# Sample attention: keys turned in 32x32 blocks by VectorE instead of by matmuls, and products with the queries stationary

## The chip, the core and the metric

The kernel runs on one core of a Trainium2 chip. The metric is the device time of one execution in microseconds. Engine names follow the profile: PE is the matrix engine (PEld its weight loads), DVE is VectorE, ACT is ScalarE, POOL is GpSimd, SP issues DMAs.

## What is computed

The program is one step of a one-layer decoder: modulation and layer norm, one input projection, four groups of mixers, an output projection, and a mixture of 32 experts. 512 prompt tokens and 8 sample tokens (one new token for each of 8 sequences with 2048 past tokens) go through it. The change touches the attention of the 8 sample tokens alone. In the reference, cut to what matters:

```
# NSA, three branches, for q (4 heads, 64 wide), one query a sequence
s_c = q . compressed_keys - slope * distance        # 64 blocks of 32 tokens
p_c = softmax(s_c);  o_c = p_c . compressed_values
imp = p_c.sum(heads), pairs summed                  # 32 past blocks of 64 tokens
sel = top 16 of imp, blocks 0 and the last two forced
o_s = softmax(q . k[sel] - slope * distance) . v[sel]     # selected pages, 2048 + 1 keys
o_w = softmax(q . k_win - slope * distance) . v_win       # window, 512 + 1 keys
nsa = gate0 * o_c + gate1 * o_s + gate2 * o_w
# DSA
score = sum over 4 index heads of w_h * relu(qi_h . ki)   # 2048 + 1 index keys, 32 wide
sel = top 256 of score
dsa = softmax(q . k[sel] - slope * distance) . v[sel]
```

Both kernels score every key of a sequence and mask with a bias of -1e30 what isn't selected, so no key is gathered by rank.

## The kernel before

Everything here stands in one block, `block_sample_attention`, between two barriers of all engines. Two sequences make a pair (`NPAIR` = 4 pairs, index t). A pair's past tokens lie on the 128 partitions: 64 partitions a sequence, and 32 tokens along the free side of each (the index j; with the new token's row and a row of padding `JP` = 34, `JW` = 10 for the window). `cache` holds the pages of one branch as [128, 4 pairs, 34, 64 key + 64 value numbers]: first the pages of `cache_nsa_slc`, and then, in the same place, those of `cache_dsa_kv`, which POOL gathers once the values of the selected branch have been multiplied (`pv_mm` 2).

Scores of a branch are made by `keys(b, turn, product, aside)` on PE. A chunk is four tiles of 128x128. `turn` multiplies slices of the pages by the identity, so that they lie turned in PSUM (for pages two matmuls a tile, one of each 64 columns of PE, L1926 and L1927); ACT copies the 128x512 result to `KTs` (`evacuate`, L2013, released by `k_t`, and it releases by `k_ev`); `product` then loads each turned tile as the stationary operand and streams the 16 (index: 32) query columns through (L1933, L1921). Scores so stand with tokens on partitions. The four branches are index keys (9 chunks), selected pages (17), window (5), DSA pages (17).

The search for the 256th largest index score (`search(k)`, 16 steps of two bits) runs on DVE: a comparison of all scores with three candidates (L2043), a sum (L2045), a signal (`give`), a small matmul by PE that adds over partitions (`count`, L1904), and six short operations on the result (L2049 to L2056, L2042). In PE's queue nine of these counts stand behind chunks of the selected pages, one in two chunks, and seven behind chunks of the DSA pages. `softmax(b, x, J)` takes column maxima on DVE, has PE turn them and spread their result, and subtracts on DVE; ACT takes the exponential; `values(b, src, J)` multiplies by the values, 132 matmuls for a branch of pages (L1950).

Order on DVE: index scores, compressed branch, block selection, searches 0 to 8, softmax of the selected pages, softmax of the window, searches 9 to 15, `choose`, first result, softmax of DSA, second result. The constants (distances times slopes, masks, tables of the search) are made by POOL at the block's start, and a single semaphore (`s_cst`) tells that all are there.

Of the kernel before, what the change touches and what calls it, by code (L numbers as in the profile page):

```python
# [1691 lines left out]
def block_sample_attention(nc, io, G, ctx, sem, sbt):  # L1692
# [5 lines left out]
    KT = sbt(ctx, "KTs", [128, 2, 512])  # L1698
# [12 lines left out]
    S = scratch(0, 128, NPAIR, JP, 8)  # L1711
    X = scratch(0, 128, NPAIR, JP - 1)
    hit = scratch(0, 128, NPAIR, 3, JP - 1)
# [20 lines left out]
    bias = scratch(1, 128, 2, JP, 8)  # L1734
    biasW = scratch(1, 128, JW, 8)
    biasC = scratch(1, 128, 8)
    QB = scratch(1, 128, 2, NPAIR, 16)
    QIB = scratch(1, 128, NPAIR, 32)
    disti = scratch(1, 128, 3, JP)
    dist = scratch(1, 128, 3, JP)  # L1740
    half = scratch(1, 128, 2)
    halfb = scratch(1, 128, 2)
    gw8 = scratch(1, DEC, DEC, 16)
    gw = scratch(1, 128, DEC, 16)
    wm = scratch(1, 128, NPAIR, 8)
    keyscore = scratch(1, 128, NPAIR, JI)
    vc2 = scratch(1, 128, NPAIR, HD + 1)
    small = sbt(ctx, "as_small", [128, 12, 32])
    mxp, mrow, diag, sums = small[:, 0], small[:, 1, 0:1], small[0:32, 2], small[:, 3]
    rinv = small[:, 4:8]  # L1750
    impT, blkm = small[:, 8, 0:NPAIR], small[:, 8, 8:8 + NPAIR]
    Pc = small[:, 9]
    imp = scratch(0, NPAIR, 2, 40)
    imp64 = scratch(0, NPAIR, 128)
    top8 = scratch(0, NPAIR, 8)
    disti = disti.bitcast(I32)
    gate_d = nc.dram_tensor("sample_gates", (DEC, 12), F32, kind="Internal").ap()

    s_new, idx_in, cache_in, win_in = sem("s_new"), G["idx_in"], [G["slc_in"], sem("as_dsa_in")], sem("as_win_in")
    idx_new, cache_new = sem("as_idx_new"), [sem("as_slc_new"), sem("as_dsa_new")]  # L1760
    s_cst, s_zero2, s_q = sem("as_cst"), sem("as_zero2"), sem("as_q")
    k_t, k_ev, k_mm = sem("as_kt"), sem("as_kev"), sem("as_kmm")
    s_read, s_step, p_step, e_in, e_ok, pv_mm = (sem("as_" + n) for n in ("read", "vstep", "pstep", "ein", "eok", "pv"))
    gate_ok, gate_st, gate_in, one_ok = (sem("as_" + n) for n in ("gate_ok", "gate_st", "gate_in", "one_ok"))
    SEARCH = 16
    early, late = 9, SEARCH - 9
    VW = HD + 2

    tiles_of = [NPAIR * JI // 4, NPAIR * JP // 2, NPAIR * JW // 2, NPAIR * JP // 2]
    first_chunk = [0]  # L1770
    for n in tiles_of:
        first_chunk.append(first_chunk[-1] + n // 4)

    with nc.Block() as block:
        @block.sync
        def _(sp):
            for a in range(2):
                sp.dma_start(keyi[64 * a:64 * a + 1, :, PAST // 64, :],
                             io["out16"][0, a::2, 0].unsqueeze(0)).then_inc(idx_new, 16)
                sp.dma_start(cache[64 * a:64 * a + 1, :, JP - 2, :],  # L1780
                             io["out13"][0, a::2, 0].rearrange("s a d -> s (a d)").unsqueeze(0)).then_inc(cache_new[0], 16)
            sp.dma_start(gate_d, gateR[0:DEC, NT]).then_inc(gate_st, 16)
            sp.wait_ge(gate_st, 16)
            sp.wait_ge(gate_ok, 1)
# [18 lines left out]
        def _(pool):  # L1803
            g = nc.gpsimd
            L = lambda i: plink(pool, i)
            def pages(dst, table, n_sem):
                for t in range(NPAIR):
                    g.indirect_dma_start(dst(t), None, table,
                                         bass.IndirectOffsetOnAxis(ap=idx[:, t:t + 1], axis=0)).then_inc(n_sem, 16)

            L(g.iota(disti[:, 0, 0:32], pattern=[[-1, 32]], base=PAST, channel_multiplier=-32))
            L(g.iota(disti[:, 1, 0:8], pattern=[[-1, 8]], base=512, channel_multiplier=-8))
            L(g.iota(disti[:, 2, 0:1], pattern=[[0, 1]], base=PAST - 31, channel_multiplier=-32))
            L(g.memset(dist[:], 0.0))
            L(g.tensor_copy(dist[:, 0, 0:32], disti[:, 0, 0:32]))
            L(g.tensor_copy(dist[:, 1, 0:8], disti[:, 1, 0:8]))
            L(g.tensor_copy(dist[:, 2, 0:1], disti[:, 2, 0:1]))
            L(g.memset(half[:], 1.0))
# [3 lines left out]
            for i, (n, back) in enumerate(((32, 2048.0), (8, 512.0), (1, 2048.0))):  # L1822
                L(g.tensor_scalar(halfb[:, 0:1], half[:, 1:2], back, None, ALU.mult))
                L(g.tensor_scalar(dist[:, i, 0:n], dist[:, i, 0:n], halfb[:, 0:1], None, ALU.add))
            L(g.tensor_scalar(halfb[:], half[:], 1.0, -BIG, ALU.subtract, ALU.mult))
            for h in range(HEADS):
                for a in range(2):
                    c = 4 * a + h
                    hb = halfb[:, a:a + 1]
                    L(g.tensor_scalar(bias[:, 0, :, c], dist[:, 0, :], -SLOPES[2 * h], hb, ALU.mult, ALU.add))  # L1830
                    L(g.tensor_scalar(bias[:, 1, :, c], dist[:, 0, :], -SLOPES[2 * h + 1], hb, ALU.mult, ALU.add))
                    L(g.tensor_scalar(biasW[:, :, c], dist[:, 1, 0:JW], -SLOPES[2 * h], hb, ALU.mult, ALU.add))
                    L(g.tensor_scalar(biasC[:, c:c + 1], dist[:, 2, 0:1], -SLOPES[2 * h], hb, ALU.mult, ALU.add))

            for x, n in ((bias[:, 0], JP), (bias[:, 1], JP), (biasW, JW)):
                y = x[:, n - 2, :].rearrange("p (s h) -> p s h", s=2)
                L(g.affine_select(out=y, in_=y, compare_op=ALU.is_equal, fill=BIG, base=0,
                                  pattern=[[-64, 2], [0, 4]], channel_multiplier=1))
                L(g.memset(x[:, n - 1, :], BIG))
# [7 lines left out]
            L(g.memset(lead, 1.0))  # L1847
            L(g.affine_select(out=lead, in_=lead, compare_op=ALU.is_equal, fill=0.0, base=0,
                              pattern=[[-64, 2]], channel_multiplier=1))
            L(g.tensor_tensor(lead[:, 0:1], lead[:, 0:1], lead[:, 1:2], ALU.add))  # L1850
            L(g.tensor_scalar(no_key, lead[:, 0:1], -1.0, 3e38, ALU.add, ALU.mult))
# [9 lines left out]
            def ones_column(b, src):  # L1861
                pool.wait_ge(k_t, first_chunk[b + 1])
                L(g.memset(src[:, :, :, HD - 1:HD], 1.0))
                pool.sem_inc(one_ok, 1)
            pool.wait_ge(k_mm, first_chunk[1])
            L(g.memset(win[:, :, JW - 2:JW, :], 0.0))
            pool.sem_inc(s_zero2, 1)
            ones_column(1, cache)
            pool.wait_ge(pv_mm, 2)
            pages(lambda t: cache[:, t, 0:32, :].rearrange("p j x -> p (j x)"),  # L1870
                  io["cache_dsa_kv"][0].rearrange("n (s j) a d -> (n s) (j a d)", s=4), cache_in[1])
            ones_column(2, win)
            ones_column(3, cache)

        @block.tensor
        def _(pe):
            step = [0]

            def take(n=1):
                step[0] += n  # L1880
                pe.wait_ge(s_step, step[0])

            def keys(b, turn, product, aside={}):

                n = tiles_of[b] // 4
                for c in range(n + 1):
                    g = first_chunk[b] + c
                    if c < n:
                        if g >= 2:
                            pe.wait_ge(k_ev, g - 1)  # L1890
                        for u in range(4):
                            m = turn(4 * c + u, lambda q: ps[q, 4 + g % 2, u * 128:(u + 1) * 128])
                        m.then_inc(k_t, 1)
                    if c >= 1:
                        pe.wait_ge(k_ev, g)
                        for u in range(4):
                            m = product(4 * (c - 1) + u, KT[:, (g - 1) % 2, u * 128:(u + 1) * 128])
                        m.then_inc(k_mm, 1)
                    if c in aside:
                        aside[c]()  # L1900
# [14 lines left out]
            def turn_index(n, out):  # L1915
                t, j = divmod(n, JI // 4)
                return pe.transpose(out(slice(0, 128)), keyi[:, t, 4 * j:4 * j + 4, :].rearrange("p j x -> p (j x)"), ident[:])

            def product_index(n, k):
                t, j = divmod(n, JI // 4)  # L1920
                return pe.matmul(ps[:, t, j * 32:(j + 1) * 32], k, QIB[:, t], start=True, stop=True)  # L1921

            def turn_pair(src, J):
                def f(n, out):
                    t, j = divmod(n, J // 2)
                    pe.matmul(out(slice(0, 64)), src[:, t, 2 * j, 0:HD], ident[:], start=True, stop=True)  # L1926
                    return pe.matmul(out(slice(64, 128)), src[:, t, 2 * j + 1, 0:HD], ident[:], start=True, stop=True)  # L1927
                return f

            def product_pair(q, J):  # L1930
                def f(n, k):
                    t, j = divmod(n, J // 2)
# [1016 lines left out]
```

## Time and profile before

| what | value |
|---|---|
| median of 3 runs | 2214.84 us (2213.9 to 2225.81) |
| the profiled execution: its time | 2203.56 us |
| the profiled execution: span | 2201.9 us |
| PE busy | 1687.8 us, 77% of the span |
| DVE busy | 913.8 us, 41% |
| ACT busy, POOL busy | 249.7 us, 264.6 us |
| mean granted clock of PE | 0.852 |

The span runs from the first instruction to the last. A granted clock of 1.00 is 2.4 GHz for PE, 0.50 is 1.2 GHz. The shares are means over stages that come one after the other, each between barriers, so a stage is read alone: what ends last in it sets when the next begins. A row of a group of instructions gives engine, line, shapes, count, time busy and mean duration. In PE's rows each float32 matmul of the program shows as two instructions, so that 132 matmuls are 264 in a count.

### The profile page before, as it was taken

What the parts mean: (1) busy time and instruction counts of PE and PEld (TensorE: products, weight loads), DVE (VectorE), ACT (ScalarE), POOL (GpSimd) and SP (SyncE); (2) the same over time, 40 slices, a digit from 0 to 9 for tenths busy, and PEclk for the clock granted to TensorE, in tenths of its full rate; (3) what the DMA queues carried; (4) which work ended last, traced back from release to release, by engine and by line L of the source; (5) the groups of instructions that cost most, each with busy time, mean ns of one, the idle gap of its engine ahead of it and who ended that gap; (6) DMA issues with size and microseconds to landing.
All of it is one profiled execution on the core that took longest, in us unless ns stands there. A gap on an engine that the chain in (4) does not pass through costs nothing. (4 is left out here: it accounts for less than half of the span.)

```text
span 2201.9 us, 52833 instructions
## 1 busy us (share of the span) xinstructions
PE 1687.8 (77%) x21375; PEld 1212.7 (55%) x21376; DVE 913.8 (41%) x2371; ACT 249.7 (11%) x614; POOL 264.6 (12%) x504
## 2 busy tenths in 40 slices
PE   4999528849777759692799768978979988988664
PEld 3878418738446658442566445645646655655321
DVE  3000475554684432377344223423434333433218
ACT  1000201105444111000000000000000000000000
POOL 0000100021213100000111111111111111111121
PEclk9999759968578675795899988989989999999777
DMA  9731100140600140536599999999998489998983
GB/s 305 264 120 42 52 10 1 41 167 9 267 1 1 39 172 21 168 159 262 226 409 411 414 414 406 400 414 412 410 414 327 172 328 406 412 387 346 415 309 152
DMA packets 131845, 533.24 MB, mean 242 GB/s; under 512 B 19403, under 2 KB 35840, under 8 KB 97266
## 3 DMA queue, kind: packets, MB, share of 16 engines
q1 hardware_dynamic: 110218, 474.66, 54.6%
q0 software_dynamic: 19952, 56.76, 6.9%
q8 instruction: 52, 0.85, 0.2%
q10 hardware_dynamic: 1600, 0.79, 0.1%
q14 instruction: 23, 0.19, 0.0%
HBM read 509.20 MB, written 24.95 MB: 243 GB/s over the span
## 5 line engine op out<-in xcount | busy, mean ns | idle before, releaser
L2699 PE MATMUL ps<-wgu,xTm 128*32 128x256 f32 x10112 | 598.7, 394 | 93.9 <-DMA wgu<-in_moe_wgu 81.3
L2699 PEld LDWEIGHTS ps<-wgu,xTm 128*32 128x32 f32 x10112 | 398.9, 114 | 283.1 <-issue 145.8
L2767 DVE STREAM_TRANSPOSE gs<-ps 128x256 f32<-128x256 f32 x158 | 71.1, 450 | 435.6 <-PE ps L2699 435.6
L2712 PE MATMUL ps<-wd,aT 128*32 128x256 f32 x2528 | 164.9, 404 | 83.7 <-issue 44.3
L2712 PEld LDWEIGHTS ps<-wd,aT 128*32 128x32 f32 x2528 | 93.1, 114 | 152.4 <-issue 126.7
L348 PE MATMUL ps<-hT,w_ring 128*128 128x260 f32 (+2 forms) x768 | 172.8, 387 | 2.0 <-DVE hT L390 2.0
L348 PEld LDWEIGHTS ps<-hT,w_ring 128*128 128x128 f32 (+2 forms) x768 | 140.8, 184 | 32.0 <-issue 4.8
L2793 DVE COPY orow<-ps 128x256 f32 x79 | 33.6, 425 | 205.9 <-PE ps L2712 205.9
L2660 POOL COPY gidx<-rowtok 128x1 int32 (+1 forms) x79 | 14.3, 181 | 827.0 <-DVE xTm L2760 827.0
L2744 ACT ACTIVATE ones<-hx 128x128 f32<-128x128 f32 x79 | 24.5, 310 | 753.1 <-DVE hx L2771 753.1
L2656 POOL DMA_INDIRECT xg<-h_dram,gidx x79 | 78.7, 996 | 64.6 <-POOL gidx L2660 64.6
L2712 PE MATMUL ps<-mixT,aT 128*32 128x256 f32 x1312 | 79.3, 379 | 1.3 <-issue 1.3
L2769 DVE TENSOR_TENSOR hx<-gs,biasT 128x256 f32<-128x256 f32 x158 | 67.2, 425 | 22.9
L2712 PE MATMUL ps<-room,aT 128*32 128x256 f32 x1216 | 73.5, 379 | 3.1 <-issue 3.1
L736 PE MATMUL ps<-par_buf 128*128 128x128 f32 (+1 forms) x480 | 59.8, 286 | 7.5 <-DVE par_buf L1010 5.6
L736 PEld LDWEIGHTS ps<-par_buf 128*128 128x128 f32 x480 | 57.5, 200 | 9.5 <-DVE par_buf L1010 6.5
L2667 POOL DMA_DIRECT2D outbuf<-orow x79 | 59.7, 756 | 22.9 <-DVE orow L2793 15.3
L2712 PEld LDWEIGHTS ps<-mixT,aT 128*32 128x32 f32 x1312 | 50.2, 110 | 22.1 <-issue 1.8
L1462 PE MATMUL ps<-dg,Pw 128*128 128x128 f32 x240 | 44.6, 349 | 20.8 <-ACT dg L1520 16.8
L2712 PEld LDWEIGHTS ps<-room,aT 128*32 128x32 f32 x1216 | 46.4, 110 | 22.9 <-issue 4.5
L1462 PEld LDWEIGHTS ps<-dg,Pw 128*128 128x128 f32 x240 | 38.8, 248 | 36.2 <-ACT dg L1520 23.9
L1926 PE MATMUL ps<-ident,cache 128*64 128x128 f32 x272 | 49.3, 342 | 9.6 <-DMA cache<-in_cache_dsa_kv,blk_idx 9.6
(643 smaller groups left out, 2122.1 us busy)
## 6 DMA issues: line engine op xcount, KB each, us to landing
wgu<-in_moe_wgu SPq DMA_DIRECT2D x128, 2048.0 KB, 25.1
wd<-in_moe_wd SPq DMA_DIRECT2D x32, 2048.0 KB, 34.3
room<-in_moe_wd SPq DMA_DIRECT2D x16, 2048.0 KB, 31.7
mixT<-in_moe_wd SPq DMA_DIRECT2D x16, 2048.0 KB, 31.9
ada_ring<-in_w_ada SPq DMA_DIRECT2D x12, 2048.0 KB, 12.0
w_ring<-in_w_in SPq DMA_DIRECT2D x10, 1024.0 KB, 5.3
outbuf<-orow POOLq DMA_DIRECT2D x79, 128.0 KB, 8.5
outbuf<-zD SPq DMA_DIRECT2D x8, 512.0 KB
```

The costliest lines, as they stand in the source:

```text
L348: mm = pe.matmul(ps[0:w, b + a, 0:HALF], w_ring[:, n % RING_IN, k, i * 128:i * 128 + w], hT[:, k, a * HALF:(a + 1) * HALF], start=(k == 0) ...
L736: m = pe.matmul(ps[:, out_bank, h * w:(h + 1) * w], lhs(h), rhs(h), start=True, stop=True)
L1462: m = pe.matmul(ps[:, 4 + r, k * 128:(k + 1) * 128], P[:, n % 3, r, k * 128:(k + 1) * 128], dg[:, n % 2, r, :], start=True, stop=True)
L1926: pe.matmul(out(slice(0, 64)), src[:, t, 2 * j, 0:HD], ident[:], start=True, stop=True)
L2656: nc.gpsimd.indirect_dma_start(xg[:], None, h_rows, bass.IndirectOffsetOnAxis(ap=idx, axis=0))\
L2667: pool.dma_start(rows4(G["outbuf"][ds(c * SLOTS, SLOTS), :]), orow[:, ds((c & 1) * 256, 256)]).then_inc(r_st, 16)
L2699: m = pe.matmul(ps[32 * c:32 * c + 32, p, 0:256].rearrange("r (s j f) -> r s j f", s=2, j=4), xT[:, k, :], blocks[:, :, p, :, c, :], start ...
L2712: m = pe.matmul(ps[32 * c:32 * c + 32, 6, 0:256], aT[:, k, :], wd[b][k // 4][:, k % 4, 256 * c:256 * c + 256], start=(k == 0), stop=(k == ...
L2744: nc.scalar.activation(sg[p], hx[:, p, 0:4, :], ACT.Sigmoid, scale=1.702).then_inc(sg_ok, 1)
L2767: v.transpose(gs[:, p], ps[:, p, 0:256]).then_inc(gu_ev, 1)
L2769: TT(h, gs[:, p].rearrange("p (a n) -> p a n", a=8), b, ALU.add).then_inc(t_rd, 1)
L2793: v.tensor_copy(orow[:, ds((g & 1) * 256, 256)], ps[:, 6, 0:256]).then_inc(r_ev, 1)
```

## The change

Names: `JK` = 33, `JN` = 9, `WK` = 33*32 = 1056, `WN` = 288. DVE now turns the keys with its transpose of 32x32 blocks, straight from the pages into SBUF (`turn_pages`, one instruction of 128x2112 a pair of sequences; the index keys 128x1056; the window 128x576). A block turn leaves each 32 tokens in their own 32 partitions, so a pair's keys come to lie as four quadrants of 32 partitions (kb). PE holds 32 query columns of a quadrant (`QB`, `QIB`, zeros between them so that the four pairs add up in one accumulation) and streams up to 512 columns of keys, four tiles at the positions (0,0), (32,32), (64,64) and (96,96) of the array, all four writing different partitions of one bank. Scores so stand with (pair, sequence, head) on partitions and tokens along the free side; one maximum a row, and the subtraction goes into ACT's bias. What follows (values, search) wants tokens on partitions, so probabilities and index scores are turned back by DVE. The selected branch is finished ahead of the search, so the DSA gather is released before it. The window's keys are turned in search 0, the DSA pages in searches 8 to 11. Constants come in five portions of `s_cst`. In the diff `parts` is ((0, 512), (512, 512), (1024, 32)), `AFTER_WIN` is 5 and `DSA_FROM` is 8.

```diff
+            def index_product(t):
+                pe.wait_ge(k_t, IDX0 + t + 1)
+                for m, (c0, n) in enumerate(parts):
+                    for kb in range(4):
+                        p = slice(32 * kb, 32 * kb + 32)
+                        x = pe.matmul(ps[p, m, 0:n], QIB[p, 32 * t:32 * t + 32], KT[p, t, c0:c0 + n],
+                                      start=(t == 0), stop=(t == NPAIR - 1), tile_position=(32 * kb, 32 * kb))
+                x.then_inc(k_mm, 1)
+            def key_product(unit, kind, bank, keys, J):
+                t = unit % NPAIR
+                pe.wait_ge(k_t, unit + 1)
+                k4 = keys.rearrange("p (j d k) -> p j d k", d=2, k=32)
+                for m, j0 in enumerate(range(0, J, 16)):
+                    n = min(16, J - j0)
+                    for d in range(2):
+                        for kb in range(4):
+                            p = slice(32 * kb, 32 * kb + 32)
+                            q0 = 256 * kind + 64 * t + 32 * d
+                            x = pe.matmul(ps[p, bank + m, 0:32 * n].rearrange("p (j k) -> p j k", k=32),
+                                          QB[p, q0:q0 + 32], k4[p, j0:j0 + n, d, :],
+                                          start=(t == 0 and d == 0), stop=(t == NPAIR - 1 and d == 1),
+                                          tile_position=(32 * kb, 32 * kb))
+                x.then_inc(k_mm, 1)
...
-            keys(1, turn_pair(cache, JP), product_pair(0, JP), {2 * i + 1: count for i in range(early)})
-            softmax_steps()
-            values(1, cache, JP)
...
+            for k in range(SEARCH):
+                count()
+                if k < NPAIR:
+                    window_product(k)
+                if k == AFTER_WIN:
+                    maximum()
+                if k == AFTER_WIN + 1:
+                    values(2, win, JN)
+                if DSA_FROM <= k < DSA_FROM + NPAIR:
+                    page_product(DSA0 + k - DSA_FROM, 1)
...
-            evacuate(0)
-            exp(0, Pc)
-            evacuate(1)
+                nc.scalar.activation(S[:, 0:n], S[:, 0:n], ACT.Exp, bias=mxc[:, 1:2]).then_inc(e_ok, 1)
...
+            def turn_pages(unit, src):
+                t = unit % NPAIR
+                L(v.transpose(KT[:, 2 * (t % 2):2 * (t % 2) + 2].rearrange("p q n -> p (q n)").rearrange("p (j x) -> p j x", x=HD),
+                              src[:, t, 0:JK, 0:HD]))
+                v.sem_inc(k_t, 1)
...
+            def softmax(n):
+                L(v.tensor_reduce(mxc[:, 0:1], S[:, 0:n], AX.X, ALU.max))
+                give()
+                take()
+                L(v.tensor_reduce(mx32, ps[0:1, 6, 0:128].rearrange("p (k c) -> p c k", c=32), AX.X, ALU.max))
+                give()
+                take()
+                L(v.tensor_copy(mxc[:, 1:2], ps[:, 6, 128:129]))
                 v.sem_inc(e_in, 1)
+            def turn_probabilities(b, n):
+                v.wait_ge(e_ok, b + 1)
+                v.wait_ge(pv_mm, b)
+                L(v.transpose(Pt2[:, 0:n], S[:, 0:n]))
+                v.sem_inc(pt_ok, 1)
...
+            v.wait_ge(k_mm, WIN0)
+            L(v.scalar_tensor_tensor(S, dflat, sl_nsa, scores(3, WK), ALU.mult, ALU.add))
+            s32 = S[:, 0:1024].rearrange("p (j k) -> p j k", k=32)
+            L(TT(s32, s32, Mk.unsqueeze(1).broadcast_to((128, 32, 32)), ALU.add))
+            softmax(WK)
+            turn_probabilities(1, WK)
```

On PE, ahead of the softmax of the selected pages, stood 17 chunks of this kind, with nine counts between them (the first rows, before); `cache` are the pages, `KTs` the turned keys, `zD` the queries, and L1904 is a count of the search.

```order
L1926 MATMUL ps<-ident,cache 64x128
L1927 MATMUL ps<-ident,cache 64x128
L1933 MATMUL ps<-zD,KTs 128x16 x4
L1904 MATMUL ps<-zA 128x12
L1926 MATMUL ps<-ident,cache 64x128
```

In their place stand, in the change, four products of 24 matmuls each (`qN` is where the stationary queries lie now), the block mask (L2005), the maximum (L1965, L1968), and the values right behind:

```order
L1937 MATMUL ps<-KTs,qN 32x512 x16
L1937 MATMUL ps<-KTs,qN 32x32 x8
L2005 MATMUL ps<-zA,zD 32x32 x4
L1937 MATMUL ps<-KTs,qN 32x512 x16
L1937 MATMUL ps<-KTs,qN 32x32 x8
L1937 MATMUL ps<-KTs,qN 32x512 x16
L1937 MATMUL ps<-KTs,qN 32x32 x8
L1965 MATMUL ps<-ident,zD 1x128
L1968 MATMUL ps<-as_small 32x1 x4
L1976 MATMUL ps<-cache,zD 8x65 x132
```

So the counts have left this place, and the values of the selected branch come before the first of them. On DVE, from the block selection to the first search, the change has these rows; L2065 turns pages, L2214 turns the index scores back, L2134 the probabilities.

```order
L2065 STREAM_TRANSPOSE KTs<-cache 128x2112 x2
L2214 STREAM_TRANSPOSE zD<-zA 128x1056
L2216 COPY qN<-ps 128x32
L2217 COPY zD<-zD 128x1
L2218 COPY zD<-zD 128x1
L2219 TENSOR_REDUCE zA<-zD 128x33x4
L2221 TENSOR_SCALAR zA<-zA 128x4
L2225 SCALAR_TENSOR_TENSOR zA<-zD,ps 128x1056
L2228 TENSOR_TENSOR zA<-zA,qN 128x1024
L2122 TENSOR_REDUCE zD<-zA 128x1
L2125 TENSOR_REDUCE as_small<-ps 1x32
L2128 COPY zD<-ps 128x1
```

Before, DVE went from the block selection straight to the first search:

```order
L2182 COPY as_small<-ps 128x4
L2043 TENSOR_TENSOR zA<-zA 128x396
L2045 TENSOR_REDUCE zA<-zA 128x12
L2049 TENSOR_SCALAR zA<-ps 128x12
L2053 TENSOR_SCALAR zA<-ps 128x4
```

The turning of two of the four pairs, the bias, the mask and the maximum have so moved ahead of the search, onto DVE.

## Rows read from the trace of the kernel before

**Rows 1.** Timeline of DVE in the stage: start, duration, engine, line, operation, wait ahead.
```profile
699.94 0.24 DVE L2119 TENSOR_TENSOR zD<-gateR,ident 8x96 f32<-8x96 f32 x1 [0.90 <-PEq L136]
...
729.75 1.32 DVE L2146 TENSOR_SCALAR zD<-zD 128x16 f32<-128x16 f32 x2 [25.04 <-POOLq L1859]
...
784.27 2.11 DVE L2189 SCALAR_TENSOR_TENSOR zA<-ps,as_small,zD 128x272 f32<-128x272 f32 x4
...
906.24 0.73 DVE L2087 COPY mixT<-ps 64x8 f32<-64x8 f32 x4 [0.45 <-PE ps L1913]
```

**Rows 2.** Who waited for whom, 740 to 910 us: total, times, longest.
```profile
DVE zA L2049 <- PE ps L1904: 61.3, 16, 15.5
```

**Rows 3.** Groups by form, 740 to 908 us: busy, mean ns.
```profile
L1927 PE MATMUL ps<-ident,cache 128*64 128x128 f32 x272 | 49.3, 343 | 0.0
```

**Rows 4.** Busy time by stretch: length, PE, PEld, DVE, ACT, POOL, clock, DMA, GB/s.
```profile
704.10:727.90 23.80, 23.80 (x115) 23.50 (x115) 0.57 (x2) 5.37 (x9) 16.97 (x90) 0.50 0.00 1
...
749.50:783.40 33.90, 33.90 (x393) 30.88 (x392) 15.95 (x57) 9.16 (x16) 0.34 (x1) 1.00 0.01 2
841.70:873.60 31.90, 31.90 (x209) 28.99 (x206) 8.39 (x32) 4.78 (x8) 0.00 (x0) 0.50 0.00 1
444.20:449.00 4.80, 4.30 (x66) 3.73 (x66) 0.42 (x1) 0.00 (x0) 0.00 (x0) 0.50 1.05 419
449.20:455.80 6.60, 2.08 (x9) 1.50 (x9) 3.96 (x5) 0.00 (x0) 0.00 (x0) 1.00 0.29 99
...
2132.20:2147.80 15.60, 14.15 (x16) 2.35 (x16) 1.27 (x1) 2.52 (x5) 11.21 (x13) 0.50 0.53 171
```

**Rows 5.** Timeline of POOL, SP and PE at the stage's start.
```profile
701.32 0.57 SPq L1778 DMA_DIRECT2D winidx<-out  x1
...
704.10 1.94 PE L1917 MATMUL ps<-ident,winidx 128*128 128x128 f32 x8 [3.10 <-DMA winidx<-out]
...
722.23 6.96 POOL L1856 MEMSET zA<- 128x1 int32 x45
```

**Rows 6.** Groups by form over the whole trace.
```profile
L2699 PE MATMUL ps<-wgu,xTm 128*32 128x256 f32 x10112 | 598.7, 394 | 93.9 <-DMA wgu<-in_moe_wgu 81.3 <-DVE xTm L2760 10.5 <-issue 0.8
...
L2760 DVE STREAM_TRANSPOSE xTm<-xg 128x256 f32<-128x256 f32 x80 | 35.0, 437 | 8.3 <-DMA xg<-h_dram,rowtok 8.3
```

**Rows 7.** Timeline of PE at four places of other stages.
```profile
343.01 3.57 PE L736 MATMUL ps<-par_buf 128*128 128x128 f32 x16 [2.56 <-DVE par_buf L1010]
...
444.23 3.73 PE L830 MATMUL ps<-vec,ST 64*64 64x64 f32 x64 [0.39 <-DVE ST L1045]
...
627.38 2.08 PE L1445 MATMUL ps<-kI,qI 32*128 32x512 f32 x4
...
911.07 7.13 PE L2362 MATMUL ps<-room,mixT 128*128 128x512 f32 x16
```

**Rows 8.** Timeline of DVE: block selection, first and last; a search step with PE free.
```profile
741.59 0.28 DVE L2167 COPY zA<-ps 4x128 f32<-4x128 f32 x1 [0.52 <-PE ps L1974]
...
744.66 0.41 DVE L2179 COPY zA<-zA 4x64 f32<-4x64 f32 x2
...
780.34 0.17 DVE L2049 TENSOR_SCALAR zA<-ps 128x12 f32<-128x12 f32 x1 [2.08 <-PE ps L1904]
...
783.47 0.17 DVE L2049 TENSOR_SCALAR zA<-ps 128x12 f32<-128x12 f32 x1 [0.95 <-PE ps L1904]
```

**Rows 9.** Timeline of ACT, PE and DVE around the last values.
```profile
897.78 1.11 ACT L2006 ACTIVATE zA<-zA 128x1088 f32<-128x1088 f32 x1 [14.19 <-DVEq L2111]
898.94 5.56 PEld L1950 LDWEIGHTS ps<-cache,zA 128*8 128x8 f32 x251 [3.28 <-ACT zA L2006]
...
905.30 0.17 DVE L2220 RECIPROCAL zA<-ps 128x1 f32<-128x1 f32 x1 [7.61 <-PE ps L1950]
```

**Rows 10.** Timeline of POOL and PE: the DSA gather and the first tile of it.
```profile
800.93 1.08 POOL L1808 DMA_INDIRECT cache<-in_cache_dsa_kv,blk_idx  x1 [19.20 <-PE ps L1950]
...
828.24 0.47 PE L1926 MATMUL ps<-ident,cache 128*64 128x128 f32 x1 [9.55 <-DMA cache<-in_cache_dsa_kv,blk_idx]
```

More of the change, by code:

```diff
@@ L1821, in _ @@
             L(g.tensor_scalar(half[:, 0:1], half[:, 1:2], -1.0, 1.0, ALU.mult, ALU.add))
[L1822 to L1825, printed above, removed]
+            L(g.tensor_scalar(halfb[:, 0:1], half[:, 1:2], float(PAST), None, ALU.mult))
@@ L1832, in _ @@
[L1832 to L1839, printed above, removed]
+                    L(g.tensor_scalar(biasC[:, 4 * a + h:4 * a + h + 1], dist0, -SLOPES[2 * h], halfb[:, a:a + 1],
+                                      ALU.mult, ALU.add))
@@ L1877, in _, with take @@
             step = [0]
-            def take(n=1):
-                step[0] += n
+            def take():
+                step[0] += 1
                 pe.wait_ge(s_step, step[0])
[L1883 to L1900, printed above, removed]
+            def index_product(t):
[6 more added lines that the diff above has]
+                x.then_inc(k_mm, 1)
@@ L1939, in softmax_steps @@
                 take()
-                pe.matmul(ps[:, 6, 128:160], ones[0:32, :], diag, start=True, stop=True).then_inc(p_step, 1)
-                if total:
-                    take()
-                    pe.matmul(ps[:, 6, 160:192], ones[:], sums, start=True, stop=True).then_inc(p_step, 1)
+                for kb in range(4):
+                    m = pe.matmul(ps[32 * kb:32 * kb + 32, 6, 128:129], mx32, minus, start=True, stop=True)
+                m.then_inc(p_step, 1)
             def values(b, src, J):
-                pe.wait_ge(e_ok, b + 1)
+                pe.wait_ge(pt_ok, b)
@@ L2191, in _ @@
[L2191 to L2202 removed]
+            v.wait_ge(k_mm, SLC0 + 1)
@@ new lines, in _ @@
+            between = {0: window_turns}
+            for t in range(NPAIR):
+                between[DSA_FROM + t] = lambda t=t: dsa_turn(t)
+            between[AFTER_WIN + 1] = lambda: turn_probabilities(2, WN)
+            for k in range(SEARCH):
+                search(k, between.get(k))
+                if k == AFTER_WIN:
+                    v.wait_ge(k_mm, DSA0)
+                    L(v.scalar_tensor_tensor(S[:, 0:WN], distW.rearrange("p j k -> p (j k)"), sl_nsa, scores(0, WN),
+                                             ALU.mult, ALU.add))
+                    softmax(WN)
@@ L2212, in _ @@
             results(2)
-            v.wait_ge(k_mm, first_chunk[4])
-            v.wait_ge(pv_mm, 3)
-            for t in range(NPAIR):
-                L(TT(S[:, t], ps[:, t, 0:8 * JP].rearrange("p (j c) -> p j c", c=8), bias[:, 1], ALU.add))
-                L(TT(S[:, t], S[:, t], keyscore[:, t, 0:JP].unsqueeze(2).broadcast_to((128, JP, 8)), ALU.add))
-            softmax(3, S, JP)
+            v.wait_ge(k_mm, DSA0 + NPAIR)
+            L(v.scalar_tensor_tensor(S, dflat, sl_dsa, scores(3, WK), ALU.mult, ALU.add))
+            L(TT(S, S, MT, ALU.add))
+            softmax(WK)
+            turn_probabilities(3, WK)
             v.wait_ge(pv_mm, 4)
@@ L2222, in _ @@
             results(4)
+AFTER_WIN = 5
+DSA_FROM = 8
 SLOTS = 32
```

435 lines of the change are left out of this document (230 added, 205 removed).

## The prediction

> **What bounds the kernel now.** I first placed the stage in the span with DVE's timeline: it runs from 699.94 to 906.97 us, 207 us [rows 1], and ends at a barrier, so what it loses or gains moves everything behind it by as much. Then I asked who is waited for. The search's 16 reads of the count (L2049) waited 61.3 us for PE, one of them 15.5 us [rows 2]. A search step whose count meets an idle PE takes 783.47 - 780.34 = 3.13 us, of which DVE waits 0.95 [rows 8]; 16 of them would be 50 us. PE by contrast is busy without a gap in the stretches of page chunks, 33.9 of 33.9 us and 31.9 of 31.9, while DVE works about half and a quarter of them [rows 4]. Turning by the identity alone shows 272 instructions on each of two column halves for 49.3 us [rows 3]. So PE bounds the page stretches, DVE with its exchanges the rest, and in between the stage waits for the DSA gather: PE sat 9.55 us until it landed at 828.24 [rows 10]. At the start DVE stood 25.04 us, for POOL's last constant by name [rows 1], but PE's index chunks filled the same time (23.8 of 23.8 us) [rows 4], so the constants alone cost next to nothing.
>
> The granted clock is part of the price. The same page chunks ran at 1.00 (2.4 GHz) in one stretch and at 0.50 (1.2 GHz) in another, both with PE busy throughout [rows 4].
>
> **Prices.** DVE: a block turn of 128x256 takes 0.437 us [rows 6], an operation of 12 columns 0.17 [rows 8], so (0.437 - 0.17)/244 = 1.09 ns a column. That gives 2.5 us for a turn of 2112, 1.3 for 1056 columns (turn, sum, maximum or bias), 0.8 for 576, 0.5 for 288. No row turns 2112 columns; I find no reason for another slope.
>
> PE: a page product is, in PE's own instructions, 8 passes of 512 columns on each of the four tiles, and 4 of 32. A 512-column pass of the whole array takes 7.13/16 = 0.45 us at full clock; the experts' four column tiles at once take 598.7/10112 x 4 = 0.24 us for 256 columns, 0.47 for 512 [rows 6, 7]; two row tiles at once at half clock take 2.08/2 = 1.0 us [rows 7]. If the four tiles run together, a product costs 8 x 0.45 to 0.47, and some 0.3 for the short ones: 4.0 us at full clock, and about 8 at half. An index product is half of that, a window product (4 passes of 288 columns) 1.1 and 2.3.
>
> Do four tiles in different rows and columns of the array run together when they write one bank? The nearest rows are matmuls of 64x64 tiles at (0,0) and (64,64) into one bank (L830): 64 passes of 64 columns in 3.73 us, 58 ns each. One whole-array pass of 128 columns at the same clock took 3.57/16 = 0.22 us, half of it for 64 columns is 0.11 [rows 7]. So two of them ran at a time. I take the same for four.
>
> The Trainium skill says otherwise: by TensorEngine Tiling (Array Packing), Restrictions and Gotchas, different row tiles cannot access the same PSUM bank simultaneously. The two tiles of L830 speak against it, at other partitions of the bank; no row here shows four. By the rule the products would take turns, which is the third case below.
>
> **The path of the change**, at full clock during products, in trace times of before.
>
> 1. Index keys. SP issues their second row at 701.32 now, and PE starts 2.8 us later [rows 5]. The row moves ahead of a selected one (0.6 us): about 703.5. Four turns of 1.3 us and their links, 708.9. Meanwhile POOL: its short memsets cost 6.96/45 = 0.155 us [rows 5], 32 of them and four long ones make the tables ready near 707, the compressed bias near 712, the distances (two ramps of 256 and 1024, up to 3 us) near 719, everything near 730. DVE is there at 710, 712, 730 and 738, so POOL costs nothing unless it is 8 us late. The compressed softmax passes PE three times behind an index product of 2 (half clock: 4) us: index done at 722.5.
> 2. Selected pages. PE: 723 + two products = 731, the mask, two more, 740.5. DVE beside it: second page turned 725, index scores out 726.5, block selection 3.5 us [rows 8] 730, two turns 735, scores turned back and summed, 738.5. So PE ends last, by 2 us.
> 3. Bias, mask, maximum: three passes over 1056 columns, 4.0; two exchanges with PE 1.7; the exponential 1.11 (1088 columns now [rows 9]) and a hand-over, 1.4; turned back 1.3: 748.9. The 132 matmuls of values stay as they are, 898.94 to 905.30, 6.4 us [rows 9]: 755.3. Before, they ended at 800.5, 0.4 ahead of the gather's issue [rows 10].
> 4. The gather's first tile came 27.7 us after that [rows 10]: now 783.0. DVE gets to search 8 after eight steps of 3.13 us, the window's softmax (3.0) and its turn (0.5): 784.3. The two meet, so the 9.55 us wait is gone, and 1.3 us is all the slack.
> 5. Searches 8 to 11. The next count stands behind a page product, so a step costs product + 0.5 instead of 3.13: first turn 2.5, a first product partly at half clock 6.5, then 4.5 each: 807.3. Four short steps, 817.7.
> 6. `choose` with its exchange 5; mask turned 2.6; first result 2.7; bias, mask, maximum 4.0; exchanges 1.7; exponential 1.4; turn 1.3; values 6.4; last result 906.97 - 905.30 = 1.7 [rows 1, 9]. Sum 26.8: 844.5.
>
> That is 62.5 us ahead of 906.97. The sum leaves out small hand-overs; as an estimate, about 100 of them are new or moved, at 0.03 to 0.05 each like the gaps between DVE's rows, so I take 57. Of it, before and after: to the first result on selected pages (800.5 to 755.3) 45, the rest by the gather's wait and the shorter DSA stretch. Nothing outside the stage changes. 2203.56 - 57 = 2146.6 for a profiled execution; the median of the three runs stands 11.3 above that execution, so 2214.84 - 57 = 2158.
>
> Costed at nothing: ACT's 16 small copies of queries (0.2 each, from 700.6, not wanted before 723); the window's four turns (3.2 us) lie beside the values in search 0; if values came sooner, they would cost that.
>
> **The rivals.** (a) *Full clock in dense products*, as above. After L830, dense for 3.7 us on two diagonal tiles, the clock went from 0.50 to 1.00 [rows 4, 7].
>
> (b) *Half clock throughout.* Four 32x32 tiles are a quarter of the array. A single small tile streamed 14.15 of 15.6 us and stayed at 0.50, and page chunks stayed there for 31.9 us [rows 4]. Then PE is the bound: pages end at 758 instead of 740.5 (+17.5, with the index products), searches 8 to 11 cost 2.5 + 4 x 8.5 = 36.5 instead of 23 (+13.5). Gain 57 - 31 = 26, with the first products perhaps quicker 29: 2186.
>
> (c) *The four tiles take turns* (the other side). A product is then 32 passes of 0.47 and short ones, 15.6 us even at full clock. Index products 30 us, done at 735; pages until 797.5 (+57); window steps +6; searches 8 to 11 67 instead of 23 (+44). 57 - 107 = 50 slower: 2265. This decides as soon as a page product takes over 4 + 57/8 = 11 us, since eight of them lie on the path. The Trainium skill's rule named above asks for this case.
>
> (d) *DVE's turns cost double* for pages read in runs of 64, 5 us each: pages +5 behind PE, searches +8, index +5: gain about 38, inside the span of (a) and (b). With a POOL table late as well it might shrink to nothing.
>
> **Chances.** (a) 0.54, (b) 0.33, (c) 0.05, (d) 0.08. The number is (a)'s: 2158; its own range 2142 to 2174. For 8 in 10 both (a) and (b) must be in: 2138 to 2190. 0.5% is 11 us, about what three runs tell apart here. Faster: all of (a) and (b), most of (d), 0.92; same 0.03; slower 0.05.
>
> **What would show it.** Stage 145 us long instead of 207. Four passes of 512 columns starting within a few hundredths, L1937 busy near 4 us for 24 matmuls; 8 at clock 0.50 is (b), 15 is (c). DVE's L2065 near 2.5 us. POOL's second gather issued near 756, and DVE waiting little or not at all for it at search 8. L2080 waiting 0.95 in searches 1 to 5 and 12 to 15. Wrong I would be above all by the clock, or if the turns or the waits on POOL's five portions put DVE behind PE.

## The result and the profile after

The changed kernel takes 2138.3 us (median of 4 runs, 2135.87 to 2141.68) against 2215.47 for the kernel before on the same chip: ratio 0.963, 95% interval [0.958, 0.968]. That is 77 us less, where 57 were forecast. The time stands at the very bottom of the range (2138); as a ratio, 0.963, it is just below it (2138 / 2214.84 = 0.965). Profiled execution against profiled execution it is 2203.56 to 2135.92, 67.6 us.

All of it comes from the stage. I measure it from DVE's first instruction in the block to its last: 207.0 us before [rows 1], 138.7 after (704.05 to 842.72). What is left of the execution's time, called the rest below, is 1996.5 and 1997.3.

DVE's timeline of the changed kernel at the places that answer to [rows 1, 8, 10] (start, duration, engine, line, operation, wait ahead):

```profile
704.05 0.22 DVE L2137 MEMSET qN<- 128x192 f32 x1 [0.97 <-PEq L136]
...
716.85 0.19 DVE L2165 TENSOR_TENSOR as_small<-ps,zD 128x32 f32<-128x32 f32 x1 [1.64 <-POOLq L1854]
...
722.07 0.19 DVE L2174 TENSOR_TENSOR as_small<-as_small,ps 128x32 f32<-128x32 f32 x1 [3.69 <-PE ps L1990]
...
734.37 4.90 DVE L2065 STREAM_TRANSPOSE KTs<-cache 128x2112 f32<-128x2112 f32 x2 [0.18 <-PE ps L1937]
...
744.33 1.31 DVE L2225 SCALAR_TENSOR_TENSOR zA<-zD,ps 128x1056 f32<-128x1056 f32 x1 [1.41 <-PE ps L1937]
...
785.52 2.38 DVE L2065 STREAM_TRANSPOSE KTs<-cache 128x2112 f32<-128x2112 f32 x1 [1.26 <-DMA cache<-in_cache_dsa_kv,blk_idx]
790.37 2.38 DVE L2065 STREAM_TRANSPOSE KTs<-cache 128x2112 f32<-128x2112 f32 x1
...
807.23 0.17 DVE L2080 TENSOR_SCALAR zA<-ps 128x12 f32<-128x12 f32 x1 [1.91 <-PE ps L1952]
809.96 0.17 DVE L2080 TENSOR_SCALAR zA<-ps 128x12 f32<-128x12 f32 x1 [0.54 <-PE ps L1952]
812.88 0.17 DVE L2080 TENSOR_SCALAR zA<-ps 128x12 f32<-128x12 f32 x1 [0.75 <-PE ps L1952]
...
841.98 0.74 DVE L2118 COPY mixT<-ps 64x8 f32<-64x8 f32 x4 [0.45 <-PE ps L1961]
```

A turn of 128x2112 costs 2.38 us. The long waits for the count (61.3 us, [rows 2]) are gone; 10.6 us are left (total, times, longest, 704 to 843 us):

```profile
DVE zA L2080 <- PE ps L1952: 10.6, 12, 1.9
```

DVE waits 1.26 us for the gather, so the search just meets it. The first two DSA turns start 4.85 us apart (the second and the third 5.40, the last two 4.85), and DVE works through all of it but short waits: it sets the pace there, as e5 shows below.

PE's timeline of the same execution (answers to [rows 7, 9]):

```profile
726.92 7.32 PE L1937 MATMUL ps<-KTs,qN 32*32 32x512 f32 x96
...
752.41 6.15 PE L1976 MATMUL ps<-cache,zD 128*8 128x65 f32 x264 [2.92 <-DVEq L2135]
...
761.73 1.17 PE L1937 MATMUL ps<-kvT,qN 32*32 32x288 f32 x16
...
764.66 2.14 PE L1937 MATMUL ps<-kvT,qN 32*32 32x288 f32 x16
...
788.01 5.08 PE L1937 MATMUL ps<-KTs,qN 32*32 32x512 f32 x48 [3.03 <-DVEq L2067]
...
793.34 3.76 PE L1937 MATMUL ps<-KTs,qN 32*32 32x512 f32 x48
```

Two page products take 7.32 us, 3.7 each. The same window product takes 1.17 or 2.14 us, and the first DSA product 5.08 where the next takes 3.76. Busy time by stretch goes with it (columns as in [rows 4]; the clock stands ahead of the last two). The first row is that of two page products, the second that of searches 0 to 8 with the window's products, the third that of the DSA products behind the first:

```profile
726.90:734.20 7.30, 7.30 (x104) 2.34 (x96) 6.44 (x22) 0.00 (x0) 4.80 (x44) 1.00 0.70 280
...
758.90:784.30 25.40, 13.14 (x159) 7.33 (x159) 17.83 (x62) 0.53 (x1) 4.59 (x5) 0.59 0.94 380
...
790.80:807.20 16.40, 14.79 (x188) 5.47 (x180) 12.62 (x24) 0.00 (x0) 0.33 (x1) 1.00 0.01 2
```

The products of the selected pages, and those of the DSA pages from the second on, ran at 1.00. Between them the mean clock was 0.59: the first two window products ran at 1.00, the last two at 0.50. The first DSA product (788.0 to 793.1) had 0.73.

### The profile page after: what moved, and what is told of

The parts are those of the page before. It is cut to its first block and busy times, and to the rows that moved or that the text cites. A ratio compares the mean times of both kernels' runs of the same rounds, so it can differ in the third digit from the quotient of the medians.

```text
span 2133.6 us, 51812 instructions
## 1 busy us (share of the span) xinstructions
PE 1622.6 (76%) x20898; PEld 1116.4 (52%) x20899; DVE 936.7 (44%) x2347; ACT 224.8 (11%) x582; POOL 266.1 (12%) x515
## 5 line engine op out<-in xcount | busy, mean ns | idle before, releaser
L2757 PE MATMUL ps<-wgu,xTm 128*32 128x256 f32 x10112 | 607.1, 398 | 100.4 <-DMA wgu<-in_moe_wgu 88.0
L2802 ACT ACTIVATE sg<-hx 128x128 f32<-128x128 f32 x79 | 24.4, 309 | 266.2 <-DVE hx L2829 266.2
## 6 DMA issues: line engine op xcount, KB each, us to landing
wd<-in_moe_wd SPq DMA_DIRECT2D x32, 2048.0 KB, 34.4
```

Source lines behind the costliest of these rows:

```text
L2757: m = pe.matmul(ps[32 * c:32 * c + 32, p, 0:256].rearrange("r (s j f) -> r s j f", s=2, j=4), xT[:, k, :], blocks[:, :, p, :, c, :], start ...
L2802: nc.scalar.activation(sg[p], hx[:, p, 0:4, :], ACT.Sigmoid, scale=1.702).then_inc(sg_ok, 1)
```

## The experiments

The stage's length is read as above, each in the profiled execution of its kernel.

| kernel | median us | ratio to before, interval | stage us |
|---|---|---|---|
| changed kernel | 2138.3 | 0.963 [0.958, 0.968] | 138.7 |
| e1 tiles one after the other | 2343.5 | 1.061 [1.055, 1.068] | 344.6 |
| e2 old products, new order | 2216.5 | 1.004 [1.000, 1.008] | 208.2 |
| e3 new products, search first | 2162.3 | 0.980 [0.974, 0.986] | 162.3 |
| e4 second index product earlier | 2138.9 | 0.968 [0.963, 0.974] | 139.2 |
| e5 turns twice | 2158.0 | 0.971 [0.965, 0.978] | 157.0 |
| e6 filler | 2139.3 | 0.963 [0.956, 0.969] | 141.0 |
| e7 four moves of order | 2131.5 | 0.959 [0.954, 0.964] | 134.7 |
| e8 four in a row | 2138.4 | 0.962 [0.956, 0.968] | 139.0 |
| e9, e10 before again | 2207.9, 2211.4 (one run each) | | 207.1, 212.9 |
| e11 e7, DSA turns from search 9 | 2131.5 | 0.961 [0.957, 0.966] | 131.9 |

**e1: do the four tiles run side by side?**

```diff
-                for m, j0 in enumerate(range(0, J, 16)):
-                    n = min(16, J - j0)
-                    for d in range(2):
-                        for kb in range(4):
+                for kb in range(4):
+                    for m, j0 in enumerate(range(0, J, 16)):
+                        n = min(16, J - j0)
+                        for d in range(2):
```

(and `kb` outermost in the index product).

> The changed kernel with the same matmuls in another order: all of tile (0,0), then all of (32,32), and so on, so that neighbours in PE's queue are never on different tiles but at three borders. If four tiles only run together because they alternate in the queue, a page product costs 24 matmuls in turn, about 8 x 4 passes of 0.45 us and 16 short ones, near 15 us at full clock instead of the 3.75 measured: index products +5 each on the path (+20), four page products +47, window +6, searches 8 to 11 about +11 each (+45), so about 115 us more than the changed kernel, near 2250, slower than before. This is also what rival (c) gave for the change itself. If instead the short product of 3.75 us came from cheap small tiles and not from running side by side, or if the queue lets later tiles overtake, the order doesn't matter: within 5 us of the changed kernel's 2138.

It took 205 us more, where 115 were expected. PE's timeline (the first row is an index product, the second two page products less three records, the third a window product, the last a DSA product):

```profile
705.92 8.86 PE L1923 MATMUL ps<-KTs,qN 32*32 32x512 f32 x24
...
743.57 54.92 PE L1937 MATMUL ps<-KTs,qN 32*32 32x512 f32 x93
...
873.81 2.16 PE L1937 MATMUL ps<-kvT,qN 32*32 32x288 f32 x16
...
897.19 27.74 PE L1937 MATMUL ps<-KTs,qN 32*32 32x512 f32 x48 [3.06 <-DVEq L2067]
```

and busy time by stretch:

```profile
897.20:924.80 27.60, 27.60 (x48) 6.10 (x48) 4.35 (x8) 0.00 (x0) 0.00 (x0) 0.50 0.00 1
```

The same 48 instructions take 27.7 us and not 3.7. A factor of four is the turn-taking; the other two is the clock, 0.50 though PE was busy without a gap. The sum had only the first factor. So in the changed kernel the tiles do run together, into one bank. With a single small tile at work the clock stayed at 0.50; the page products with four at work had 1.00.

**e8: how many may stand in a row?** (`kb` and `d` exchanged, so that a tile gets four instructions in a row.)

> The changed kernel with another order of the matmuls of a page product: within a block of 512 columns both halves of the key on one tile, then the next tile. Each tile so gets four instructions in a row, and not two; with all twelve pairs of a tile in a row the product took 27.7 us and not 3.75, but the window's product of four in a row took no longer than before. If the instructions of a tile wait in a queue of its own that holds four, four in a row cost nothing: 3.75 us a product, 2138. If tiles only run together when neighbours in the queue differ, or when the whole queue of about four holds all of them, a product takes 1.5 to 2 times as long at least (6 to 8 us): 4 x 2.5 on the pages and as much in searches 8 to 11, 10 to 30 us slower.

```profile
737.33 7.46 PE L1937 MATMUL ps<-KTs,qN 32*32 32x512 f32 x96 [2.27 <-DVEq L2067]
```

7.46 for 7.32, and 2138.4 for 2138.3 in the median: four in a row cost next to nothing. One rule fits all four shapes: a tile's instructions wait for their tile, up to four of them, and the next tile's begin once no more than four stand ahead. Four in a row: side by side (e8, and e1's window, 2.16 us). Six in a row at half clock: a tile works 3.5 us, the next begins when two of 0.85 are through, 3.5 + 3 x 1.8 = 8.9 (8.86 measured). Twelve in a row, of which the last four are the short ones: one after the other, 27. The starts in e1's trace say the same: the second tile's first instruction starts within 0.01 us of the first tile's third where six stand in a row (707.63), and of its ninth where twelve do (750.40). The rule is an estimate, fitted to these runs; e8 is the only run made for it, and five in a row, for one, was not tried.

**e2 and e3: order and products apart.** e2, in the kernel before:

```diff
-            keys(1, turn_pair(cache, JP), product_pair(0, JP), {2 * i + 1: count for i in range(early)})
+            keys(1, turn_pair(cache, JP), product_pair(0, JP))
             softmax_steps()
             values(1, cache, JP)
+            for i in range(early):
+                count()
```

with the nine searches behind `softmax(1, S, JP)` on DVE.

> The kernel before with the new order alone: nine searches behind the softmax and the values of the selected pages, old identity turns and old products. If order and products each bring a part by itself, the gather's wait of 9.55 us goes and the time falls by up to 10 us, to about 2205. The rival, which I hold likelier: the order brings nothing without the cheap products, since the nine counts cost nothing where they stood (PE was busy with chunks and DVE idle there), and behind the values they take 9 x 3 = 27 us in which PE idles; the window's chunks then come 25 us later. Selected values end at about 798, searches until 825, window until 840, DSA chunks from there instead of 828: 8 to 14 us slower than before, 2223 to 2229.

Stage 208.2, 1.2 more than before, not 8 to 14. This execution (2206.1) is one of the quicker of ten: the median is 8.9 us above that of the 13 runs of the kernel before beside it (2216.5 against 2207.5), and the ratio's interval reaches from no change to 0.8% slower. Where DVE reads the window's scores, in e2 and in the kernel before:

```profile
843.94 1.07 DVE L2197 TENSOR_TENSOR zA<-ps,zD 128x80 f32<-128x80 f32 x4 [17.61 <-PE ps L1933]
```

```profile
810.51 1.07 DVE L2196 TENSOR_TENSOR zA<-ps,zD 128x80 f32<-128x80 f32 x4 [17.63 <-PE ps L1933]
```

From the stage's start that is 30.5 us later, where some 25 were expected; the window's chunks ran at 0.50 in e2 (827 to 843 us) and at 0.94 before (804 to 812). The first count among the DSA chunks is read 20.5 us later. What gave this back was the clock. A search step beside two DSA chunks, in DVE's timeline of e2 and of the kernel before:

```profile
869.17 0.17 DVE L2051 TENSOR_SCALAR zA<-ps 128x12 f32<-128x12 f32 x1 [2.08 <-PE ps L1904]
873.43 0.17 DVE L2051 TENSOR_SCALAR zA<-ps 128x12 f32<-128x12 f32 x1 [2.08 <-PE ps L1904]
```

```profile
857.05 0.17 DVE L2049 TENSOR_SCALAR zA<-ps 128x12 f32<-128x12 f32 x1 [5.70 <-PE ps L1904]
864.92 0.17 DVE L2049 TENSOR_SCALAR zA<-ps 128x12 f32<-128x12 f32 x1 [5.69 <-PE ps L1904]
```

4.26 against 7.87 us. In e2 the DSA chunks ran at 1.00 for 34 us, before for 10 of them. From the first of the seven reads beside them to the last, e2 takes 25.6 us and the kernel before 39.8; with the exchange behind them 18 us come back. My sum had no such term. So the order alone brought nothing here, and in this execution the clock gave back nearly all that the order cost. Why the clock rose in e2 stays open.

e3, in the changed kernel: nine counts and searches ahead of the selected pages' softmax, the window's products and softmax between, `DSA_FROM = 9`.

> The changed kernel's products with nearly the old order: nine searches ahead of the softmax of the selected pages, the window's softmax behind its values, seven searches last, with the DSA pages turned from search 9. Products alone. Selected pages: index done at the same time, products done beside the searches, searches 0 to 8 end about 738 + 9 x 2.8 = 763, selected values end near 780, the gather lands 27 us later, near 806, while DVE is through with the window at 790: a wait of 12 to 19 us, then searches 9 to 15 (33 us) and the last 26.5: about 866, 20 to 25 us more than the changed kernel's 843.5, so near 2160. If the order were worth nothing (the rival), the time would stay within 5 us of 2138; if it is worth what step 1 of my sum put on the gather's wait alone, 10 us.

Stage 162.3, 23.6 more, with DVE's wait for the gather as expected:

```profile
807.86 2.38 DVE L2065 STREAM_TRANSPOSE KTs<-cache 128x2112 f32<-128x2112 f32 x1 [18.12 <-DMA cache<-in_cache_dsa_kv,blk_idx]
```

By the stages read, products alone bring 44.7 us, order alone -1.2 (with the clock's help), order on top of the new products 23.6: it pays only once the searches stand beside the gather and no longer beside chunks that hid them.

**e4: one wait taken away.** `index_product(1)` ahead of the transpose of `mxp` on PE.

> The changed kernel with the second index product ahead of the compressed branch's first transpose in PE's queue. PE there waits for DVE, which waits for a constant of POOL; then DVE waits 3.7 us for the second index product. If PE's queue order is what delays the index part, the product fills PE's idle time and the whole stage comes 2.5 to 3.7 us earlier (stage 139.1 to about 136). If POOL's constant or the third and fourth product set the end of the index part, it brings under 1 us. The median can't tell this apart from nothing (0.15%), the stage's rows can.

The 3.69 us wait fell to 0.55, and DVE came to the block selection 1.9 us earlier within the stage. PE then:

```profile
722.72 7.32 PE L1937 MATMUL ps<-KTs,qN 32*32 32x512 f32 x96
...
732.79 9.02 PE L1937 MATMUL ps<-KTs,qN 32*32 32x512 f32 x96 [2.26 <-DVEq L2067]
```

The last two products took 9.02 us and not 7.32. Busy time by stretch, in e4 and in the changed kernel:

```profile
730.30:742.00 11.70, 9.24 (x104) 2.81 (x104) 8.12 (x9) 0.00 (x0) 2.50 (x23) 0.85 0.01 4
```

```profile
734.40:744.30 9.90, 7.52 (x104) 2.43 (x104) 8.05 (x8) 0.00 (x0) 1.34 (x11) 1.00 0.01 2
```

The mean clock is 0.85 against 1.00, behind an idle time of the same 2.26 us, and the stage was 139.2. The gain was gone. Why the clock fell here and not there stays open.

**e5: is DVE the bound where it turns?** (each `turn_pages` transpose done twice)

> The changed kernel with each of DVE's eight turns of 128x2112 done twice (2.38 us more each), nothing else. If DVE sets the pace wherever pages are turned, all of it lands on the end but the 1.4 us for which DVE waits for the last selected product: pages +8.4 us, searches 8 to 11 +9.8, the gather moves along with the selected values: about 18 us more, near 2156. The rival, that PE or the gather sets the pace in one of the two places and hides the second turn there, gives +8 to +10, near 2147; the price that the prediction put on turns of double cost (its rival d) was 13 for the two places.

19.7 us in the median, 18.3 in the stage: eight turns of 2.38 are 19.0. All but 0.7 us of them shows in the stage, so DVE is the bound in both places.

**e6: filler for the clock.**

```diff
+            def filler(n):
+                for _ in range(n):
+                    pe.matmul(ps[:, 2, 0:128], ident[:], ident[:], start=True, stop=True)
...
+                elif k < DSA_FROM and k != AFTER_WIN + 1 or k >= DSA_FROM + NPAIR:
+                    filler(FILL)
...
+FILL = 5
```

> The changed kernel with five idle matmuls of 128x128 behind each count that has nothing else behind it (searches 4, 5, 7, 12 to 15): 1.1 us of PE at full clock, 2.2 at half, in the 2.3 us in which PE waits for DVE; their result isn't used. If the half clock of PE is what makes DVE wait 0.75 us for a count and not 0.54, and PE at work keeps the clock up, these steps fall from 2.93 to 2.72 us, the first DSA product from 5.1 to 3.7, exchanges of a softmax by 0.1 each: 3 to 4 us less in all. If the clock stays low with fillers on it, the fillers stand in front of the counts: no gain, or 0.2 to 1 us more a step, up to 5 us slower. The medians will hardly tell; the steps in the trace do.

The hope was refuted. With PE busy for 18.0 of 24.0 us the clock stayed at 0.50:

```profile
764.00:788.00 24.00, 17.98 (x157) 13.13 (x157) 15.89 (x49) 0.53 (x1) 0.92 (x2) 0.50 0.96 397
```

One search step more than in the changed kernel had the 0.54 us wait (three, not two). The stage became 2.3 us longer, 1.5 of it in the first DSA product, 6.55 us and not 5.08.

**e7 and e11: the waits together.** e7 makes four moves: POOL makes the compressed bias ahead of the tables, DVE picks the slopes later, `index_product(1)` as in e4, the third page is turned ahead of the block selection. e11: the same and `DSA_FROM = 9`.

> The changed kernel with four moves of order alone: POOL makes the compressed branch's bias ahead of the tables, DVE picks the slope columns later, the second index product stands ahead of the first transpose on PE, and the third page is turned ahead of the block selection. If DVE's waits for POOL (1.6 us), for the second index product (3.7) and for the last page product (1.4) are real parts of the path, the selected pages end 4 to 6 us earlier, and since the gather starts behind them, the stage is that much shorter: 139.1 to about 134, near 2133. The rival is what the second index product alone did: the pages end 0.2 us earlier and the stage stays at 139, since PE, idle for longer in between, runs its last page products at half clock (9.0 us for two and not 7.3).

> The kernel with the four moves of order (2131.48 us, stage 134.65), and the DSA pages turned from search 9 on and not 8. There DVE waits 1.38 us for the gather ahead of the first turn. If the gather is only that much late, a further search step of 2.9 us ahead of it covers the wait and the stage becomes 1.4 us shorter, 133.3. If the last of the searches were bound by something else, by the product behind the count, it stays at 134.7. The median can't tell (0.07%); the stage's rows can.

e7: stage 134.7, 4.0 shorter, median 2131.5 against 2138.4 for e8 and 2139.3 for e6 beside it. In DVE's timeline the wait of 1.41 is 0.37, 5.9 us earlier in the stage (34.4 for 40.3 from its start):

```profile
736.20 1.31 DVE L2225 SCALAR_TENSOR_TENSOR zA<-zD,ps 128x1056 f32<-128x1056 f32 x1 [0.37 <-PE ps L1937]
...
777.10 2.38 DVE L2065 STREAM_TRANSPOSE KTs<-cache 128x2112 f32<-128x2112 f32 x1 [1.38 <-DMA cache<-in_cache_dsa_kv,blk_idx]
```

A first DSA product of 6.62 us, where the changed kernel has 5.08, took back 1.5 of them. e11: stage 131.9, 2.7 less where 1.4 was expected: the wait of 1.38 is gone, and the first product took 5.52, 1.1 less. Its median, 2131.5, is that of e7: the rest was 3.7 us longer in the execution read. Both beat the kernel before and, by 7 us, the changed one.

**e9, e10: where does the spread of the kernel before come from?**

> The kernel before once more, for a second profiled execution. Its runs spread from 2201 to 2239 us and the changed kernel's from 2136 to 2142. If the spread comes from where PE's granted clock falls in the stretches of page chunks (33.9 us at 1.00 in the first, 31.9 us at 0.50 in the second of the execution read), this one has its chunks at another mixture of 1.00 and 0.50, and its stage differs from 207.0 by several us as that mixture says, while the rest stays within 3 us of 1996.5. If the spread comes from elsewhere (the experts' transfers), the stage is 207 again and the rest differs.

> The same kernel a third time, for the same purpose: with three executions the two parts, the stage and the rest, can be set against the clock of the chunks. Theory: the stage between 195 and 225 us by the share of the chunks at 0.50, the rest near 1997. Rival: the stage 207, the rest different.

The rests are 2000.8 and 1998.5, the stages 207.1 and 212.9 (the first execution: 1996.5 and 207.0). e9 came out as the rival said, the stage unchanged and the rest 4.3 us longer; e10 as the theory said. In e10 the DSA chunks were at 1.00 for 3 us and not 10; its second step waits 3.99 us where the first execution has two of 2.08:

```profile
840.41 0.17 DVE L2049 TENSOR_SCALAR zA<-ps 128x12 f32<-128x12 f32 x1 [3.99 <-PE ps L1904]
848.29 0.17 DVE L2049 TENSOR_SCALAR zA<-ps 128x12 f32<-128x12 f32 x1 [5.70 <-PE ps L1904]
```

So the stage moved by 5.8 us along with the clock's pattern, but the rest moves by 4 too. Over the 35 runs beside the experiments (2201 to 2241 us) time and mean granted clock go together (correlation -0.91; 0.845 at 2201, 0.829 at 2241). No profile is of a run above 2212, so where the slow ones lose it stays open.

## Why the prediction was right or wrong

The case was the forecast one, (a): faster, full clock in the dense products. The mechanism held and the size was 20 us short: 10.7 in the profiled execution (2146.6 forecast, 2135.9 measured), 8.9 in its step to the median. Three terms of the sum failed: the allowance of 5.5 us for hand-overs, where the stage shows none beyond what the rows already held; the search step, put at 3.13 us and measured at 2.73 to 2.93; and the step from the profiled execution to the median, put at 11.3 us and measured at 2.4.

Step by step, from the stage's start:

| until | forecast | measured |
|---|---|---|
| 1 index done | 22.6 | 22.4 |
| 2 pages done | 40.6 | 40.1 |
| 3 values done | 55.4 | 54.5 |
| 4 first DSA turn | 84.4 | 81.5 |
| 5 count 12 read | 107.4 | 103.2 |
| end of short steps | 117.8 | 112.5 |
| 6 end | 144.6 + 5.5 | 138.7 |

Up to the end of the selected values the stage takes 54.5 us, where it took 100.6 before (800.5 less 699.94): 46 of the 68 us, forecast 45. The rest comes behind them.

- **The hand-over allowance, 5.5 us, was wrong**: half of the miss in the profiled execution. Without it the sum ends at 144.6, still 5.9 above the measured 138.7, so no such gaps are left over beside the durations and waits that the rows gave. By its own figures (100 gaps at 0.03 to 0.05 us) it would have been 3 to 5. The sum without it would have given 62.5.
- **The search step, 3.13 us, was too long**: 2.93 with the count at half clock, 2.73 at full (waits 0.75 and 0.54). The row it came from [rows 8] has a wait of 0.95, longer than with PE idle; PE wasn't free there as I took it. Eight such steps brought DVE to the first DSA turn 25.7 us behind the selected values, not 29.0 (the forecast's own terms add up to 28.5). There it waited for the gather, which was 27.0 us behind them, not 27.7. So step 4 was 2.0 us shorter than forecast, and the four short steps behind count 12 were 1.0 shorter.
- **Page products**: 3.7 us, forecast 4.0; searches 8 to 11 took 21.7, not 23.0. The turns were 2.38 (2.5 forecast), the last stretch 26.2 (26.8). The prices from the far rows [rows 6, 7] held within a tenth.
- **Step 1 came out right by luck.** DVE's wait for POOL (1.64) was in no step, so "POOL costs nothing" didn't hold. The wait for the second index product (3.69) was in the sum, as the pass behind a product of 4 us at half clock. Against them, the four index turns were through 8.0 us into the stage, not 9.0. e7 takes both waits away along with two other moves and is worth 4.0 us together; POOL's part alone isn't shown.
- **The median**: the 11.3 us between the profiled execution and the median of before was carried over to the changed kernel, which has 2.4. Its runs spread over 6 us, those of before over 40 (all 35). That is 8.9 us of the miss, and nothing of the mechanism. Why before's rest spreads is open, as said above; its chunk stretches are one part (e2, e10).
- **Rival (c)**: the four tiles don't take turns. The Trainium skill's TensorEngine Tiling (Array Packing), Restrictions and Gotchas, says that different row tiles cannot access the same PSUM bank simultaneously; the trace disagrees, with 3.7 us a product for four tiles in one bank and 27.7 in e1 when they do take turns. e1 also shows that (c) was priced too low: with turn-taking by order the clock stayed at 0.50, 27.7 us a product and not 15.6, 2343 and not 2265.
- **Rival (b)**: not in the page products, but half clock held in part of what the sum called full or mixed: the window products from the third on (2.14), part of the first DSA product, most counts of the search. Few of them lie on the path. (b) also calls four tiles of 32x32 a quarter of the array; by area they are a sixteenth (4 x 1024 of 16384). No number of it hangs on that.
- **Rival (d)**: turns cost 1.1 ns a column also in runs of 64. Had they cost double, e5 shows 18.3 us in the stage, not the 13 that I gave the two places.

## What to carry to other kernels

Price products and order apart and then together: here an order that brought nothing with the old products is worth 24 us with the new ones. Take a step's duration from a row with no other work beside it, and don't add an allowance for gaps that the row already has. A wait that you remove may come back through PE's clock: look at the granted clock of the next stretch before you count the gain.

## What the runs showed of the hardware

- Four 32x32 tiles at (0,0), (32,32), (64,64) and (96,96) ran side by side into one bank and lost nothing: 3.7 us for eight passes of 512 columns each and four short ones at clock 1.00; a pass of 512 of the whole array takes 0.45 [rows 7].
- How far small tiles overlap hung on how many instructions in a row one tile got: four overlapped fully (7.46 us for two products, e8), six in part (8.86 us, e1; an index product takes 3.74 in the changed kernel at the same clock), twelve hardly or not (27.7 us, e1).
- In e1 two instructions of the first index product start 0.006 us apart at 707.63, where those of one tile start 0.85 apart. So the second tile's first starts there, ahead of the first tile's fourth at 708.48 (the records name no tile). The Trainium skill's TensorE: Matmul & The Clock Gate, The mechanism (under Packing small matmuls), has matmuls start in strict program order; these starts disagree.
- The clock stayed at 0.50 with one small tile at work without a gap (27.6 of 27.6 us, e1) and with PE busy for 18.0 of 24.0 us, whole-array fillers among it (e6). With four small tiles at once it was at 1.00 in the page products, while the window products from the third on ran at 0.50 and took 2.14 us, not 1.17. The same whole-array chunks, with PE busy throughout, stayed at 0.50 before [rows 4] and ran at 1.00 in e2.
